# A chunked recurrence on one core: the first product moved to another PSUM bank, the solve and a mask moved ahead

## The reference, cut to what matters

```python
def step(state, inp):                       # per direction d and head h, state 64 x 64
    r_t, w_t, k_t, v_t, a_t, b_t = inp
    sa = jnp.einsum('dbhij,dbhj->dbhi', state, a_t)
    state = (state * w_t[..., None, :] + sa[..., :, None] * b_t[..., None, :]
             + v_t[..., :, None] * k_t[..., None, :])
    y = jnp.einsum('dbhij,dbhj->dbhi', state, r_t)
    return state, y
...
y = ys[0] + jnp.flip(ys[1], axis=1)
mu = jnp.mean(y, axis=-1, keepdims=True)
var = jnp.mean(jnp.square(y - mu), axis=-1, keepdims=True)
y = ((y - mu) * lax.rsqrt(var + GN_EPS)).reshape(bsz, t, c) * lnx_w + lnx_b
out = (y + bonus.reshape(bsz, t, c)) * g
```

## Time and profile before

| | us |
|---|---|
| median of three timed runs | 1623.55 |
| the three runs | 1619.76, 1623.55, 1632.7 |
| the profiled execution | 1613.03 |
| its span, first to last instruction | 1611.1 |
| TensorE busy in the span | 1540.1 (96%) |
| VectorE busy | 1065.5 (66%) |
| ScalarE busy | 732.5 (45%) |
| the mean granted TensorE clock | 0.992 of full |
| the recurrence (the stretch 1212 to 1350) | 138 |

### The profile page before, as it was taken

How to read it: one execution, slowest core, us unless ns; L and a number is a source line. 1 busy time by engine, 2 the same in 40 slices (tenths; PEclk the granted TensorE clock), 3 DMA queues, 4 the chain that set the end, 5 groups by cost and what they waited for, 6 DMA issues and landing times.

```text
span 1611.1 us, 35745 instructions
## 1 busy us (share of the span) xinstructions
PE 1540.1 (96%) x15477; PEld 1479.2 (92%) x15477; DVE 1065.5 (66%) x1285; ACT 732.5 (45%) x814; POOL 69.6 (4%) x51
## 2 busy tenths in 40 slices
PE   7999999998999999999998999999988899999998
PEld 7999999887999999999988999999866778999997
DVE  5776487764766547765577776476767775877446
ACT  5443345542534335333455433364564434455333
POOL 2000000100100001000101000021000000100000
PEclk9999999999999999999999999999999999999999
DMA  8565545201555556655533665554300012565552
GB/s 273 183 198 193 191 150 174 89 2 54 182 184 182 184 185 186 200 187 201 179 119 105 186 201 187 196 190 158 127 31 3 3 55 77 172 195 185 198 195 79
DMA packets 155064, 243.25 MB, mean 151 GB/s; under 512 B 9283, under 2 KB 106174, under 8 KB 154814
## 3 DMA queue, kind: packets, MB, share of 16 engines
q1 hardware_dynamic: 154510, 240.63, 45.8%
q10 hardware_dynamic: 432, 0.79, 0.2%
HBM read 240.34 MB, written 1.05 MB: 150 GB/s over the span
## 4 chain that ended last, share of the span: by engine, by line
PE 87%; DVE 8%; ACT 3%; issue 2%; DMA 1%; POOL 0%; SPq 0%; ACTq 0%; DVEq 0%
PE dense_ps L2495 24%; PE dense_ps L2496 24%; PE dense_ps L2497 24%; PE mixer_ps L450 1%; DVE w_lo L2865 1%; PE mixer_ps L538 1%; PE dense_ps L450 1%; PE mixer_ps L1755 1%; PE mixer_ps L1183 1%; PE mixer_ps L1174 0%; DVE xT L2983 0%; DVE x_raw L622 0%; DMA raw<-in_ffn_w_gu 0%; ACT score_b L1213 0%; ACT w_hi L2692 0%
## 5 line engine op out<-in xcount | busy, mean ns | idle before, releaser
L2865 DVE TENSOR_TENSOR w_lo<-raw,w_hi 128x2048 fp32r<-128x2048 f32 x225 | 523.1, 2336 | 240.6 <-ACT w_hi L2692 239.7
L2495 PE MATMUL dense_ps<-h_hi,w_hi 128*128 128x256 f32 x2368 | 665.1, 281 | 11.7 <-DVE h_lo L2940 8.1
L2497 PE MATMUL dense_ps<-h_hi,w_lo 128*128 128x256 f32 x2368 | 658.9, 278 | 0.0
L2496 PE MATMUL dense_ps<-h_lo,w_hi 128*128 128x256 f32 x2368 | 658.9, 278 | 0.0
L2692 ACT ACTIVATE w_hi<-raw 128x2048 fp32r<-128x2048 f32 x225 | 428.7, 1914 | 330.9 <-DMA raw<-in_ffn_w_down 115.1
L2495 PEld LDWEIGHTS dense_ps<-h_hi,w_hi 128*128 128x128 f32 x2368 | 448.7, 189 | 17.8 <-issue 17.3
L2496 PEld LDWEIGHTS dense_ps<-h_lo,w_hi 128*128 128x128 f32 x2368 | 446.7, 189 | 0.8 <-issue 0.5
L2497 PEld LDWEIGHTS dense_ps<-h_hi,w_lo 128*128 128x128 f32 x2368 | 446.7, 189 | 0.0
L2495 PE MATMUL dense_ps<-g_hi,w_hi 128*128 128x256 f32 x960 | 265.8, 277 | 0.0
L2496 PE MATMUL dense_ps<-g_lo,w_hi 128*128 128x256 f32 x960 | 265.8, 277 | 0.0
L2497 PE MATMUL dense_ps<-g_hi,w_lo 128*128 128x256 f32 x960 | 265.8, 277 | 0.0
(11 more groups left out here) (553 smaller groups left out, 1777.0 us busy)
## 6 DMA issues: line engine op xcount, KB each, us to landing
raw<-in_ffn_w_gu SPq DMA_DIRECT2D x176, 512.0 KB, 4.7
raw<-in_ffn_w_down SPq DMA_DIRECT2D x88, 512.0 KB, 4.0
raw<-in_w_ff SPq DMA_DIRECT2D x64, 512.0 KB, 4.2
raw<-in_w_in SPq DMA_DIRECT2D x36, 512.0 KB, 4.3
raw<-in_a_w_in SPq DMA_DIRECT2D x32, 512.0 KB, 4.4
raw<-in_a_w_out SPq DMA_DIRECT2D x8, 512.0 KB, 4.1
raw<-in_b_w_in SPq DMA_DIRECT2D x8, 512.0 KB, 4.1
raw<-in_b_w_out SPq DMA_DIRECT2D x8, 512.0 KB, 4.1
```

Source lines behind the costliest of these rows:

```text
L2495: pe.matmul(o, hi, mh, start=start, stop=False)
L2496: pe.matmul(o, hi, ml, start=False, stop=False)
L2497: return pe.matmul(o, lo, mh, start=False, stop=stop)
L2865: dve.tensor_tensor(w_lo[:, p % SLOTS, :], raw[:, p % SLOTS, :], w_hi[:, p % SLOTS, :].bitcast(F32), ALU.subtract).then_inc(lo_ready, 1)
```

## The change

Five edits, all in the recurrence.

1. TensorE: the product with the values goes to `D_ps` bank 2. The two waits on `inv_up` that closed `inverse(i)` are moved to the head of the first solve, behind the wait for `w_sys`, so the product no longer waits for the inverse's last copies. Ahead of it stand the waits that free `D_ps` bank 2: `r_ssm` at i + 2 (sets 0 to 2) and `r_rv` at i (sets 1 to 3).
2. TensorE: `solve(0)` runs ahead of quarter 0.
3. ScalarE: the first copy to `w_sys` reads `D_ps` bank 2.
4. VectorE: `finished(i - 1)` goes from the last level of the inverse to behind the masks of the apply, and `solved(i, 0)` stands ahead of `masked(i + 1, 0)`.
5. VectorE: `masked(i + 1, 3)`, and then `finished(i - 1)`, stand ahead of `solved(i, 1)`.

```diff
--- before.py
+++ after.py
@@ -1737,8 +1737,6 @@
                 pe.wait_ge(r_yk, i)
             inverse4_pe(pe, lambda s_: GRAM[i % 2][:, s_, 0:P], X_R[i % 2], XT_R[i % 2], ly_r,
                         [(r_g, 4 * i + 4), (r_init, i + 1)], GROUPS_A + i, beside, between)
-            for half in range(2):
-                pe.wait_ge(inv_up, 14 * (GROUPS_A + i) + 13 + half)
 
         def apply(i):
             gram_, ar_, x_, xt_ = GRAM[i % 2], AR[i % 2], X_R[i % 2], XT_R[i % 2]
@@ -1749,6 +1747,9 @@
 
             def solve(phase):
                 pe.wait_ge(r_wk, 2 * i + phase + 1)
+                if phase == 0:
+                    for half in range(2):
+                        pe.wait_ge(inv_up, 14 * (GROUPS_A + i) + 13 + half)
                 for h in range(2):
                     for d in range(2):
                         s_ = 4 * h + 2 * d + (d if phase == 0 else 1 - d)
@@ -1756,13 +1757,17 @@
                                          w_sys[:, 2 * h + d, :], start=True, stop=True)
                 last.then_inc(r_u, 1)
             pe.wait_ge(r_vtok, i + 1)
+            if i + 1 < RT:
+                pe.wait_ge(r_ssm, i + 2)
+            if i:
+                pe.wait_ge(r_rv, i)
             for h in range(2):
                 for d in range(2):
-                    last = pe.matmul(M_ps[:, 0, P * (2 * h + d):P * (2 * h + d) + P],
+                    last = pe.matmul(D_ps[:, 2, P * (2 * h + d):P * (2 * h + d) + P],
                                      gram_[:, 4 * h + 3 * d, 2 * P:3 * P], v_tok_r[:, d, :], start=True, stop=True)
             last.then_inc(r_w, 1)
+            solve(0)
             quarter(0)
-            solve(0)
             quarter(1)
             pe.wait_ge(r_bktok, i + 1)
             pe.wait_ge(r_uk, 2 * i + 1)
@@ -1986,7 +1991,7 @@
         def apply(i):
             for phase in range(2):
                 act.wait_ge(r_w, 2 * i + phase + 1)
-                act.activation(w_sys[:, :, :], banks(0, 1), ACT.Copy).then_inc(r_wk, 1)
+                act.activation(w_sys[:, :, :], banks(0, 1) if phase else banks(2, 1, D_ps), ACT.Copy).then_inc(r_wk, 1)
             if i and i + 1 < RT:
                 act.activation(XT_R[(i + 1) % 2][:, :, :], over_mid(ident, 8), ACT.Copy).then_inc(r_init, 1)
             act.wait_ge(r_y, i + 1)
@@ -2233,8 +2238,6 @@
                 if lv == 6:
                     if more:
                         key_out(i + 1)
-                    if i:
-                        finished(i - 1)
             dve.wait_ge(r_init, i + 1)
             inverse4_dve(dve, lambda half: GRAM[i % 2][:, 4 * half:4 * half + 2, 0:P], X_R[i % 2], XT_R[i % 2], GROUPS_A + i, beside)
 
@@ -2248,10 +2251,9 @@
             more = i + 1 < RT
             if i == 0:
                 dve.wait_ge(c_edge, 3)
+            solved(i, 0)
             if more:
                 masked(i + 1, 0)
-            solved(i, 0)
-            if more:
                 masked(i + 1, 1)
             dve.wait_ge(r_s, i + 1)
             for d in range(2):
@@ -2261,9 +2263,10 @@
             last.then_inc(r_sk, 1)
             if more:
                 masked(i + 1, 2)
+                masked(i + 1, 3)
+            if i:
+                finished(i - 1)
             solved(i, 1)
-            if more:
-                masked(i + 1, 3)
         dve.wait_ge(r_free, 1)
         scans(0)
         less(0)
```

## The result

| | before | after |
|---|---|---|
| median, first comparison (10 runs each) | 1623.23 us | 1609.49 us |
| the runs | 1613.75 to 1632.7 | 1605.24 to 1626.04 |
| ratio | | 0.993, 95% interval 0.9902 to 0.9958 |
| the profiled execution (span) | 1613.03 (1611.1) | 1610.78 (1608.8) |

The account below looks back on a forecast made before the run. TensorE was taken as the bound (87% of the span), with 4.8 us of touchable waits in the recurrence. Order 3.1 us plus clock 1.7 us, 4.8 us off the 1623.55 us median, gave 1618.8 us, range 1612 to 1627.5.

Parts of the forecast that it names:

- What bounds it: Whole kernel: TensorE's chain is 87% of the span; its recurrence waits for the inverse's last copies total 4.8 us.
- part 1: Apply's start: values' product begins at the inverse's last matmul's end, 1.29 us earlier in sets 0 to 2, 0.96 in set 3.
- Part 2: First solve ahead of first quarter: new 0.69 us wait replaces the 1.29 us gap, gaining 0.6 us in each of sets 0 to 2.
- Part 3: VectorE's order in the apply: solution copies precede quarter 0's mask, nothing is late, 0.9 us left at the state's product.
- Part 4: Apply's end: fourth mask and finished(i-1) before the second solve's copies; these not late, next inverse 0.1 us earlier, three times.
- rival B: Apply's end: second solve's copies come late in sets 1 and 2, no gain at the turn; 1621.4 us, chance 0.13.
- Order in all: Recurrence: gain from the order of work, 3 x 0.6 + 0.96 + 3 x 0.1 = 3.1 us.
- Part 5: Passage from inverse to apply: the one clock fall seen, in set 1, goes as the hole fills; 1.7 us more.
- The sum: Whole kernel: 3.1 us of order plus 1.7 us of clock, 4.8 us off the timed median, 1618.8 us.
- A: Recurrence: the clock falls as often as before, so the gain is 3.1 us, 1620.4 us; chance 0.30.
- D: Recurrence: the clock falls in more turns, three falls instead of one, +0.3 us, 1623.9 us; chance 0.08.
- C: Apply's start: product starts where it did, the new 0.69 us wait is bare; +1.8 us, 1625.3 us; chance 0.07.

Follow-up runs that it names:

- e4: Kernel of before with only the values' product moved to D_ps bank 2, quarter 0 still ahead of the solve: 1619.37 us, ratio 0.9968.
- e10: Changed kernel with the fourth mask and finished(i-1) back at their old places: profiled span 1614.5 us, recurrence 135.7 us.
- e5: Kernel of before with TensorE's idle hole after the inverse filled by a second, unread product with the values: ratio 1.0015.
- e6: Changed kernel with the two inv_up waits back ahead of the product, so TensorE idles there again: 1625.27 us, ratio 1.0034.
- e1: Kernel of before run again unchanged, as a control: 1622.81 us, ratio 0.9994.
- e12: Kernel of before with only the values' product moved to D_ps bank 2, profiled once more: span 1607.3 us, recurrence 140.7 us.
- e9: Changed kernel with the second chunk's values' product put into the wait before the first solve in sets 0 to 2: 1617.16 us, ratio 0.9978.
- e11: Kernel of before with the unread filler product in TensorE's hole, profiled once more: span 1618.7 us, recurrence 139.1 us.
- e7: Kernel of before, unchanged, profiled once more to count clock falls: span 1619.8 us, recurrence 145.8 us.

## Why the prediction was wrong, point by point

- **What bounds it, and part 1.** Right. The product starts at T in all sets; set 3 gained 1.00 us (0.96 said).
- **Part 2, the solve first.** Right in kind: a new wait of 0.69 us in sets 0 to 2, to the hundredth. e4 shows that this step is needed: by order the early product alone wins nothing in sets 0 to 2. The size of the gain was short. I counted "the same three pieces of work" at the same length. They are shorter. The state's product started at 1306.19 - 1300.53 = T + 5.66 before and at 1302.76 - 1297.98 = T + 4.78 now, 0.88 less, where I had 0.6. Before, quarters and solve alternate: 1.06 us from quarter 0 (1302.97) to the solve (1304.03) and 1.07 from quarter 1 to the state (1306.19). Now the two quarters stand together and take 0.97 and 0.96: 0.2 us per set. The other 0.08 is that the product starts ahead of the modelled end T.
- **Part 3, VectorE's order.** Right: nothing late, 0.75 us left at the scaled state.
- **Part 4, the tail and the turn.** The copies are not late, so rival B falls; the turn gave 0.15 and not 0.1 per set (e10 against the change: 14.71 - 14.56). By the Trainium skill's rule on the pipeline's emptying ("VectorE: DVE Perf Modes", "The DRAIN you can't avoid") they would have been 0.1 late. The trace sides with the start-to-start times: finished(1)'s first operation starts 1.25 us behind the start of a mask pair whose full duration is 1.36. The same section adds that a next operation that isn't held starts earlier; I had left that out.
- **Order in all.** 3.1 said, 4.06 measured: 0.6 by the quarters that stand together, 0.15 by the turn, the rest by the product's start.
- **Part 5, the clock. This step failed, and it makes most of the miss.** I read one profile, saw one fall in four turns, and put the clock's term of the sum at 1.7 us. In the profiles it was 5.25. The mechanism was right: the fall belongs to the hole at the turn, and it goes with it. The rate was wrong. Further profiles of before had three and four sets with a fall. The falls cost 1.6, 6.8 and 7.4 us, 5.3 on average, and a fall in set 3 cost 2.8 alone (14.72 against 11.92). As to the rule of the Trainium skill ("TensorE: Matmul & The Clock Gate", "What's actually happening"), that "the default state is throttled, and activity releases the throttle": I took from it only that a fuller turn can help. e5 and e6 agree: no fall in the filled turns, falls again with the hole put back (0.66 and 0.62 of full). How often the clock falls at such a turn it doesn't say, and that was what I had wrong.
- **The sum.** Of the 6.6 us between 4.8 said and 11.4 measured, the clock is 3.6 and the order of work 1.0. The other 2.1 no profile explains; they lie within the interval of the timed runs (6.8 to 15.9).
- **The median.** I took the profiled execution's events for those of the timed runs, 10 us slower at the median. That distance was itself the hint: the profiled execution was faster than all ten timed runs of before. One fall and few slow-paced matmuls are what set it apart from e1's. I named the distance and didn't ask what made it.
- **Rivals.** A (the clock as often as before) and D (more falls) fall with the three profiles of after, C (the product not free at T) with the timeline.
- **What stays open.** How much the place of the hole counts beside its size (e4 and e12). And whether the change also touched the pace. After had 3377, 2970 and 3254 slow-paced matmuls, before 3212, 6546 and 3769; at 4.45 ns this is 5.8 us on average, of the same size as the scatter. e5's and e9's times both lie some 7 us above what their recurrences would give. It wasn't settled whether a kernel has a pace of its own or it is luck. The same kernel shows both paces in the same stage (e5 and e11 from 680 to 740 us), so luck has at least a part.

## What to carry to other kernels

A short idle hole of TensorE that recurs in a thinly filled stretch can cost as much again by the clock as by its own length: here 4.8 us of idle in four turns came with some 5 more of lowered clock, and filling the hole with matmuls that no one reads stopped the falls in both profiles. Before pricing an event that comes in some executions and not in others, look at more than one execution, and take a distance between the profiled execution and the timed median as a question about which events that one profile lacks. And when two steps compete for the slot behind a wait, put the one first whose inputs are there: by order the early product won nothing in sets 0 to 2 until the solve stood ahead of the quarter that waited for the keys.

## What the runs showed of the hardware that I had not expected

- Dense fp32 matmuls of 128 x 256 run at one of two steady paces, 113.3 or 117.8 ns from start to start, at full granted clock and without idle; a long stage keeps one pace, and the same stage of the same kernel had the other pace in another profile (e5 and e11). The number at the slower one ran from 1523 to 7535 of some 10,800 matmuls and moved the span by up to 27 us, more than any edit here. What picks the pace wasn't found.
- Two Gram quarters (matmuls of 64 rows) behind each other take 0.97 and 0.96 us; a quarter alone between matmuls of 128 rows takes 1.06 or 1.07. Each passage from one form to the other costs about 0.1 us, and two quarters together save two of them.
- A fall of the granted clock at a turn lengthened the set by 1.4 to 1.6 us where it was short (0.72 over 6 us, e7) and by 2.6 to 2.9 where it was longer (0.66 over 10 us, e6 and set 3 of e7). No idle of TensorE at these turns was longer than 1.5 us.
- The inverse of set 3 took from 19.1 to 20.1 us between profiles, without a fall. Weight DMAs run in that stretch. This wasn't followed up.
